# Order of the first modulation blocks and an early half norm in a two-layer hybrid backbone

## What is computed

```
mod_x = silu(c) @ w_ada[l] + b_ada[l]          # 9 x 1024 values; mod_c likewise from c_ctx
h = rmsnorm(x, g) * (1 + scale) + shift        # shift = m[0], scale = m[1], gate = m[2]
x = x + 0.5 * gate * ((silu(h @ w_gate) * (h @ w_up)) @ w_down)      # w_gate: 1024 x 2816
```

## Time and profile before

| | us |
|---|---|
| median of 3 runs | 2739.49 (2739.39 to 2739.58) |
| the profiled execution | 2733.11, span 2731.3 |
| VectorE busy | 1973.8 (72%) |
| ScalarE busy | 958.2 (35%) |
| GpSimd busy | 167.3 (6%) |
| mean granted TensorE clock | 0.987 of 2.4 GHz |

### The profile page before, as it was taken

One profiled execution on the slowest core, in us unless ns is written; L12 is line 12 of the kernel. 1 busy time (PEld: TensorE's weight loads), 2 busy tenths in 40 slices (PEclk: granted clock), 3 DMA queues, 4 the chain that ended last, 5 costly groups with the idle time before them and its releaser, 6 DMA issues. The chain is left out here.

```text
span 2731.3 us, 40276 instructions
## 1 busy us (share of the span) xinstructions
PE 2606.2 (95%) x14704; PEld 2355.3 (86%) x14704; DVE 1973.8 (72%) x3138; ACT 958.2 (35%) x1674; POOL 167.3 (6%) x316
## 2 busy tenths in 40 slices
PE   6999999989997999999999999999999988999998
PEld 4899999988955889999999799999987856888886
DVE  5688888888847278888888787777768665544445
ACT  4333432332157242432332424333423264322222
POOL 2000000020003200000001000000010013100001
PEclk8999999999999999999999999999999999999999
DMA  8134333322111113333333133334313111222221
GB/s 300 43 120 132 118 92 121 111 90 95 63 46 33 32 54 101 120 95 117 108 123 111 44 105 116 105 108 126 116 43 100 62 62 32 78 92 92 92 94 61
DMA packets 190672, 256.21 MB, mean 94 GB/s; under 512 B 7262, under 2 KB 130764, under 8 KB 190540
## 3 DMA queue, kind: packets, MB, share of 16 engines
q1 hardware_dynamic: 190540, 254.43, 29.2%
HBM read 252.31 MB, written 2.10 MB: 93 GB/s over the span
## 5 line engine op out<-in xcount | busy, mean ns | idle before, releaser
L1171 PE MATMUL ps<-h_hi,w_hi 128*128 128x384 f32 (+2 forms) x2440 | 844.5, 346 | 33.2 <-DVE h_lo L2245 17.8
L1173 PE MATMUL ps<-h_hi,w_lo 128*128 128x384 f32 (+2 forms) x2440 | 837.0, 343 | 0.0
L1172 PE MATMUL ps<-h_lo,w_hi 128*128 128x384 f32 (+2 forms) x2328 | 800.9, 344 | 0.0
L1171 PEld LDWEIGHTS ps<-h_hi,w_hi 128*128 128x128 f32 x2440 | 462.8, 190 | 82.6 <-issue 24.1
L1173 PEld LDWEIGHTS ps<-h_hi,w_lo 128*128 128x128 f32 x2440 | 462.9, 190 | 31.7
L1172 PEld LDWEIGHTS ps<-h_lo,w_hi 128*128 128x128 f32 x2328 | 441.6, 190 | 29.6 <-issue 1.0
L1723 ACT ACTIVATE w_hi<-raw 128x512 fp32r<-128x512 f32 x348 | 210.1, 626 | 350.7 <-PE ps L1173 272.0
L1171 PE MATMUL ps<-t_hi,w_hi 128*128 128x384 f32 x864 | 292.7, 339 | 0.0
L1173 PE MATMUL ps<-t_hi,w_lo 128*128 128x384 f32 x864 | 292.4, 338 | 0.0
L1172 PE MATMUL ps<-t_lo,w_hi 128*128 128x384 f32 x864 | 292.2, 338 | 0.0
L2300 DVE SCALAR_TENSOR_TENSOR side_acc<-side_raw,ccol,side_acc 128x512 f32<-128x512 f32 x364 | 258.0, 745 | 7.2 <-DMA side_raw<-in_w_ada 7.0
(11 more groups left out here) (213 smaller groups left out, 3663.4 us busy)
## 6 DMA issues: line engine op xcount, KB each, us to landing
side_raw<-in_w_ada SPq DMA_DIRECT2D x240, 256.0 KB, 2.7
raw<-in_w_ffn_gate SPq DMA_DIRECT2D x44, 1024.0 KB, 5.3
raw<-in_w_ffn_up SPq DMA_DIRECT2D x44, 1024.0 KB, 5.4
raw<-in_w_ffn_down SPq DMA_DIRECT2D x44, 1024.0 KB, 5.1
raw<-in_w_in SPq DMA_DIRECT2D x14, 1024.0 KB, 5.2
ada_buf<-in_w_ada SPq DMA_DIRECT2D x12, 1024.0 KB, 12.7
raw<-in_w_out SPq DMA_DIRECT2D x8, 1024.0 KB, 5.1
raw<-in_w_in SPq DMA_DIRECT2D x8, 512.0 KB, 7.5
```

What stands on the lines that cost most here:

```text
L1171: mm(out, wh, xh, start=start, stop=False, skip_group_check=reopened)
L1172: mm(out, wh, xl, start=False, stop=False, skip_group_check=reopened)
L1173: return mm(out, wl, xh, start=False, stop=stop, skip_group_check=reopened)
```

## The change

The first blocks are loaded as 0, 2, 1, 3 (shift and scale of chunks 0 to 3 first), with the gate tile's load between the two pairs. The norm of the first layer's first network is done in two halves of four chunks (`EARLY`): reciprocals first, `first_scale(0)`, chunks 0 to 3 of both segments, then blocks 1 and 3, `first_scale(1)` and chunks 4 to 7. TensorE multiplies chunks 0 to 3 with the gate tile around blocks 1 and 3 and keeps four accumulations open; the rest of the gate follows, then the up tile with blocks 4 and 5 between its context and latent parts. Slots, buffer places and counts follow this order.

```diff
-FIRST_BLOCKS = (0, 1, 2, 3, 4, 5)
-BEFORE, BETWEEN = FIRST_BLOCKS[:4], FIRST_BLOCKS[4:]
+FIRST_BLOCKS = (0, 2, 1, 3, 4, 5)
+BETWEEN = FIRST_BLOCKS[4:]
+EARLY = KD // 2
...
+    def first_ada(self):                      # Plan
+        self.tile(("G", 0, 0))
+        for kind in ("ada", "adaT"):
+            self.slot((kind, 0, 0))
+        for i in range(3):
+            self.slot(("vec", i))
+        for s in seg_order(0):
+            self.slot(("stat", 0, s))
+        for kind in ("ada", "adaT"):
+            self.slot((kind, 0, 2))
+        for n, key in enumerate((("ada", 0, 1), ("adaT", 0, 1), ("ada", 0, 3), ("adaT", 0, 3))):
+            self.slot(key, (self.bank + 4 + n) % 8)
...
+        if f == 0:
+            keys = [(w, f, 0, c, s) for w in "gu" for s in (first, second) for c in range(2)]
...
-            for b in BEFORE[:3]:              # SyncE
+            for b in FIRST_BLOCKS[:2]:
...
             load(("G", 0, 0))
-            for half in range(2):
-                load_ada(3, half)
+            for b in FIRST_BLOCKS[2:4]:
+                for half in range(2):
+                    load_ada(b, half)
...
+            def first_pass(w, s, ks):         # TensorE
+                o, n = PIECES[s][:2]
+                wh, wl = wk((w.upper(), 0, 0), KD)
+                for k in ks:
+                    wait_h(0, k, s)
+                    for c in range(2):
+                        key = (w, 0, 0, c, s)
+                        if k == 0:
+                            wait_bank(pe, key)
+                        last = mm3(...)
+                        if k == KD - 1:
+                            last.then_inc(products, 1)
+            def first_ada():
+                pe.wait_ge(cpad_ready, 4)
+                ada_block(0)
+                turn(0)
+                ...
+                for s in seg_order(0):
+                    stat(0, s)
+                ada_block(2)
+                turn(2)
+                wait_split(("G", 0, 0))
+                first, second = seg_order(0)
+                first_pass("g", first, range(EARLY))
+                ada_block(1)
+                turn(1)
+                first_pass("g", second, range(EARLY // 2))
+                ada_block(3)
+                turn(3)
+                first_pass("g", second, range(EARLY // 2, EARLY))
...
+                def gate_up_begun():
+                    for w in "gu":
+                        if w == "u":
+                            wait_split(("U", 0, 0))
+                        for s in seg_order(0):
+                            first_pass(w, s, range(EARLY if w == "g" else 0, KD))
+                            if (w, s) == ("u", seg_order(0)[0]):
+                                ada(BETWEEN)
...
-            ada(BEFORE)                       # ScalarE
+            for s, j in square_order(0):
+                square(0, s, j)
+            ada((0,))
+            take_vector(0, vcol[:, 0, :])
+            take_vector(1, vcol[:, 1, :])
+            take_vector(2, wdw[:])
+            for s in seg_order(0):
+                root(0, s)
+            ada((2,))
+            high(0, 1, range(0, 2))
+            split(("G", 0, 0))
+            high(0, 1, range(2, EARLY))
+            ada((1,))
             act.wait_ge(lam_dot, 1)
             act_fn(lamw[:, 0:2 * DEPTH], lamw[:, 0:2 * DEPTH], ACT.Exp).then_inc(lam_exp, 1)
-            high(0, 1, (0,))
+            high(0, 0, range(0, EARLY))
+            ada((3,))
+            high(0, 1, range(EARLY, KD))
+            high(0, 0, range(EARLY, 6))
             split(("U", 0, 0))
-            high(0, 1, (1,))
-            high(0, 1, range(2, KD))
-            high(0, 0, range(0, 5))
+            high(0, 0, range(6, KD))
             ada(BETWEEN)
-            high(0, 0, range(5, KD))
...
-            ada(BEFORE)                       # VectorE
+            over_rms(0, 1)
+            over_rms(0, 0)
+            ada((0, 2))
             for i in range(4):
                 wait_freed(dve, ("vec", i))
-            shift_scale(0, 0)
-            scaled(0, 1, (0, 1))
+            first_scale(0)
+            scaled(0, 1, range(EARLY))
+            split(("G", 0, 0))
+            scaled(0, 0, range(EARLY))
+            ada((1, 3))
+            first_scale(1)
+            scaled(0, 1, range(EARLY, KD))
+            scaled(0, 0, range(EARLY, KD))
             split(("U", 0, 0))
-            scaled(0, 1, range(2, KD))
-            scaled(0, 0)
             ada(BETWEEN)
```

More of the change, by code:

```diff
@@ L253, in ada @@
     def ada(self, blocks):
-        def bank(i):
-            return (self.bank + i) % 8 if blocks is BETWEEN else None
+        bank = lambda i: (self.bank + i) % 8
         for n, b in enumerate(blocks):
[L260 to L266, removed]
             self.slot(("ada", 0, b), bank(n % 2))
@@ L324, in fast_ffn @@
         first, second = last_slots(f)
-        for key in [(w, f, 0, c, first) for w in "gu" for c in range(2)] + [(w, f, 0, c, second) for c in range(2) for w in "gu"]:
+        keys = [(w, f, 0, c, first) for w in "gu" for c in range(2)] + [(w, f, 0, c, second) for c in range(2) for w in "gu"]
+        if f == 0:
+            keys = [(w, f, 0, c, s) for w in "gu" for s in (first, second) for c in range(2)]
+        for key in keys:
             self.second_stat(f, key)
@@ L498, in build @@
                 self.slot(("vec", 3))
-        self.ada(BEFORE)
+        self.first_ada()
         for l in range(DEPTH):
@@ L589, in trunk @@
         ada_homes = [(b, half) for b in FIRST_BLOCKS for half in range(2)]
-        ada_places = [h_at, h_at + 4 * TILE, h_at + 8 * TILE, h_lo_at, h_lo_at + 4 * TILE, h_lo_at + 8 * TILE,
+        ada_places = [h_at, h_at + 4 * TILE, h_lo_at, h_lo_at + 4 * TILE, h_at + 8 * TILE, h_lo_at + 8 * TILE,
                       w_hi_at, w_lo_at, E, E + 4 * TILE, E + 8 * TILE, E + 11 * S3]
@@ L812, in hcount @@
         def hcount(q, j, s):
-            return 16 * q + 8 * seg_order(q).index(s) + j + 1
+            i = seg_order(q).index(s)
+            if q == 0:
+                return 2 * EARLY * (j // EARLY) + EARLY * i + j % EARLY + 1
+            return 16 * q + 8 * i + j + 1
         def sqcount(q, s, j):
@@ L1194, in stat, with ada_block @@
                 mm(pt(("stat", q, s), n), ones[:], sqsum[:, o:o + n], start=True, stop=True).then_inc(products, 1)
+            def ada_block(b):
+                key = ("ada", 0, b)
+                wait_bank(pe, key)
+                for k in range(KD):
+                    q, home = k % 4, (b, k // 4)
+                    if k % 4 == 0:
+                        pe.wait_ge(ada_landed[home], 16)
+                    src = ada_buf[home][:].rearrange("p (k n) -> p k n", k=4)
+                    last = mm(ps[32 * q:32 * q + 32, bank_of(key), :], cpad[:, k, :], src[:, q, :],
+                              start=(k < 4), stop=(k >= 4), skip_group_check=True)
+                last.then_inc(products, 1)
             def ada(blocks):
-                pe.wait_ge(cpad_ready, 4)
                 for n, b in enumerate(blocks):
[L1199 to L1217, removed]
+                    ada_block(b)
                     if n:
@@ L1220, in ada @@
                 turn(blocks[-1])
+            def first_pass(w, s, ks):
[6 more added lines that the diff above has]
+                        if k == 0:
+                            wait_bank(pe, key)
+                        last = mm3(pt(key, n), wh[:, k, 128 * c:128 * c + 128], wl[:, k, 128 * c:128 * c + 128],
+                                   h_hi[:, k, o:o + n], h_lo[:, k, o:o + n], k == 0, k == KD - 1, True)
+                        if k == KD - 1:
+                            last.then_inc(products, 1)
+            def first_ada():
+                pe.wait_ge(cpad_ready, 4)
+                ada_block(0)
+                turn(0)
+                pe.wait_ge(const_landed, 16 * 3)
+                turn_vector(0)
+                turn_vector(1)
+                pe.wait_ge(taps_landed, 16)
+                turn_vector(2)
+                for s in seg_order(0):
[11 more added lines that the diff above has]
+                first_pass("g", second, range(EARLY // 2, EARLY))
             def turn(b):
@@ L1326, in gate_up_first @@
                                             last.then_inc(products, 1)
-                        if f == 0 and s == 1:
-                            ada(BETWEEN)
                 def down(g, it=None):
@@ L1356, in pair @@
                         halved("U", x + 1, it)
-                gate_up_first()
+                if f:
+                    gate_up_first()
+                else:
+                    gate_up_begun()
                 g, after = NG - 1, (1, 3, 4, 6)[f]
@@ L1672, in _ @@
             pe.wait_ge(pool_const, 2)
-            ada(BEFORE)
+            first_ada()
             for l in range(DEPTH):
@@ L1752, in ada @@
                 for b in blocks:
[L1753 to L1762, removed]
                     key = ("ada", 0, b)
-                    if b == 3:
```

(17 more changed lines are left out.)

## The result

The changed kernel takes 2750.95 us (median of 6 runs, 2749.04 to 2752.56), the kernel before, measured beside it, 2739.44 (6 runs, 2734.71 to 2739.95). The ratio is 1.0044, with an interval of 1.0031 to 1.0057: slower by 8.5 to 15.6 us. The profiled execution of the changed kernel has a span of 2748.0 us.

What follows compares the result with a forecast made beforehand. TensorE, busy 95% of the span, was taken as the bound. Chained waits put T at 107.2 against 94.6 us, +12.6, which added to 2739.5 gave 2752.1, called 2752 us; range 2745 to 2760 for 8 in 10.

Steps and rivals of the forecast that it cites:

- T: First multiplication of gate tile 1, at 94.61 us in the kernel before; forecast at 107.2 us.
- Start: TensorE's start of the first gate tile: forecast at 46.1 us, 4.3 us earlier than before.
- First context chunks: Gate tile, context chunks 0 to 3 on TensorE at half clock: 5.2 us, to 51.3.
- Behind block 1: Latent chunks wait for block 1, its copy, Exp table and exponential; latent chunk 0 at 57.0 us, chunks 0 and 1 end 59.9.
- (c): Rival: clock at 1.2 GHz in the broken middle, +4 to +8 us, 2756 to 2760; chance 0.23.
- Second half of the norm: Chunks 4 to 7 on VectorE and ScalarE with the up splits: from 64.8 to 78.2 us.
- The bank wait: Turns of blocks 4 and 5 wait for Silus to free banks 2 and 3: first turn 92.4, second ends 94.4 us.
- Latent pass: Up tile's 48 latent multiplications: 10.9 us, plus 1.9 lost to half clock, ending at T.
- What hid it: Gate tile 1's low split and token sums hide under the latent pass, using nearly all VectorE's former 8.37 us idle time.
- Carried one to one: Behind T both kernels run the same instructions, so T's shift of +12.6 us reaches the end unchanged.
- (b): Rival: no bank wait, or ScalarE does its Silus in time; T 5.0 us earlier, +5.7, 2745 us; chance 0.12.
- (a): Rival: early work fills the waits and only TensorE's work counts; T = 93.0, -1.6 us, 2738; chance 0.05.

Runs made afterwards that it cites:

- d1_delay: Kernel before, with the product of block 4 computed eight times instead of once to delay T; ratio to the kernel before 1.0048.
- e1_banks: Changed kernel, but the turns of blocks 4 and 5 take banks 0 and 1, not those of the gate context products; 2739.8 us, ratio 1.0007.
- e4_all: Changed kernel, with block 1 before the gate split wait, block 3 before the latent chunks, turns in banks 0 and 1; ratio 0.9967, measured again 0.9979.
- e2: Changed kernel, but ScalarE makes latent chunks 0 to 3 before copying block 1 and takes the exponential after block 3's copy; ratio to before 1.0033.
- e3: Changed kernel, but TensorE does block 1 and its turn before it waits for the gate tile's split; ratio to the kernel before 1.0020.
- b1: Kernel before, with statistics, roots and reciprocals moved ahead of blocks 2 and 3 and the norm kept whole; ratio to the kernel before 1.0004.
- e5: As e4_all, but block 3 is multiplied between context chunks 1 and 2 and turned after chunk 3; ratio to the kernel before 0.9976.

## Why the prediction was right, and where it was not

2752.0 us was forecast and 2750.95 measured; T was forecast at 107.2 and came at 107.77. The rows show the waits of the forecast at their place: `h_hi` of latent chunk 0 behind the Exp table (53.31), the turns behind a Silu (91.20), and the up tile as VectorE's split ends (76.76; the first up multiplication at 76.82), though there TensorE hardly waited, since its last gate product started only at 76.54. The mechanism was right. That T came within 0.6 us is luck: terms of 0.7 to 1.6 us were off in both directions (in all, forecast 3.3 us too long and 3.9 too short), and they nearly cancelled.

- **Start.** 46.1 was forecast (45.5 to 47.0), 44.83 came, outside that range. The step was block 2: I took it whole at half clock and its turn at up to 1.9 us, to 37.7 or later. Half of it ran at full clock (2.98 us) and the turn took 1.05, to 36.96, so the reciprocals (to 36.98) were the bound, and the first `tn` came at 38.04 and not 39.2.
- **First context chunks.** 5.2 forecast, 4.5 measured: the clock came back at 48 us.
- **Behind block 1.** Copy, table load and exponential as forecast, 2.0 us from 51.29 to the first `h_hi`. The latent chunks 0 and 1 took 4.5 us and not 2.9, because the clock had fallen again: the first eight multiplications come every 0.43 us. That is the mechanism of rival (c), at one place, for 1.6 us.
- **Second half of the norm.** From `tn` 4 to VectorE's up split I forecast 11.1 us and 9.95 came (64.53 to 74.48). The step was the up split between latent chunks 5 and 6, and the lags that I added to it: ScalarE had made latent chunk 5 before VectorE wanted it, its split delayed VectorE by 0.1, and the lag of 0.75 was not there.
- **The bank wait.** From the end of block 5 to the first latent multiplication 6.7 forecast, 8.2 measured. The wait itself was right (the first turn at 91.20, 4.8 us after 86.41; 4.7 forecast), but the turns, at half clock, took 3.54 and not 2.0. This is the term that I had at full clock although I expected half clock for the pass right behind it.
- **Latent pass.** 12.8 forecast, 13.2 measured.
- **What hid it.** VectorE's idle time under the latent pass is 2.35 us in the changed kernel and was 8.37: the cover held, with 2 us to spare.
- **Carried one to one.** Forecast and, by d1_delay, borne out within its interval of 3.7 us either way. The profiled spans differ by 16.7 us and T by 13.2; the other 3.5 lie behind T, and the clock's part of them is 1.6 by the estimate. The medians differ by 11.5, less than T.
- **The chances.** The forecast, (c) and half of (b) add up to 0.89, not 0.88.

Rivals (a) and (b) have fallen by the trace (the waits at 54.86 and 91.20). e1_banks is what (b) would have been: 5.0 us of T above before, 5.7 forecast. Rival (a) gave T = 93.0 as the best that this order can do with nothing waited for; e4_all, the same work with blocks 1 and 3 placed otherwise, reaches 89.76, because its start is 1.4 us earlier and block 1 lies in idle time.

Of the Trainium skill's rule on tables, "ScalarE: Activation LUTs" (What ACT_TABLE_LOAD costs): both loads on the path took 1.28 us, each began 0.02 us after the instruction before it had ended (51.91 and 88.89), and the next instruction began 0.01 us after each (53.20 and 90.18). The drain of 1.38 us that the page adds for each switch is not in these rows; with it the forecast would have been 2755.

## What to carry to other kernels

When a product is cut in two so that its first half can start early, look at what stands between the halves on each in-order engine, and not only at TensorE: here one matmul block behind the first half held up ScalarE, and ScalarE held up chunks that were ready. A bank given by its distance from a rotation is tied to the order of the slots around it; when that order changes, count again who holds the bank and which engine frees it. The idle time that a new order opens (37 to 44.8 us here) is the place for the work that it displaces.

## What the runs showed of the hardware

The same gap can cost its length or more. Some 45 us behind T TensorE waits for the same thing in both kernels for the same 2.5 us (a down tile's load, its split). Windows of the kernel before, then of the changed one:

```profile
137.00:141.00 4.00, 1.76 (x11) 1.47 (x10) 1.93 (x4) 1.81 (x4) 0.00 (x0) 1.00 0.98 325
141.00:145.00 4.00, 4.00 (x23) 3.81 (x24) 3.90 (x8) 2.13 (x5) 0.00 (x0) 1.00 0.67 217
```

```profile
150.00:154.00 4.00, 1.81 (x12) 1.52 (x10) 1.98 (x4) 1.71 (x4) 0.00 (x0) 0.98 0.99 338
154.00:158.00 4.00, 4.00 (x15) 4.00 (x16) 3.90 (x8) 2.12 (x5) 0.00 (x0) 0.59 0.68 222
```

In the first the clock stays at 2.4 GHz and 23 multiplications follow in 4 us, in the second it falls after the gap and 15 follow. At this gap the clock fell in the traces of the changed kernel, e2, e3, b1 and d1 (0.57 to 0.66 in the 4 us from T + 46.3 on) and in none of before, e1, e5 and the two of e4_all (1.00). Behind T the kernel of b1 is the one before, so the fall is not the changed kernel's own; what decides it no run here shows. Two executions of one kernel can differ behind T as well: 2636.5 and 2643.0 us for e4_all. The place of T in the trace repeated within 0.3 us for that kernel, the only one profiled twice, and told the experiments apart where single times could not. It is not free of the clock either: in d1_delay half clock in the statistics moved the start by 1.0 us.
